# A two-block transformer layer on one core: output-stage tile order, routing's counts and slot table, and the first row gather

## The chip, the cores and the metric

The kernel runs as one program on one core of a Trainium2 chip. TensorE (PE) multiplies matrices, VectorE (DVE) and ScalarE (ACT) do elementwise work, GpSimd (POOL) here mostly starts indexed transfers, and SyncE (SP) starts the weight loads. The metric is the device time of one execution in microseconds (us). All data are fp32.

## The reference, cut to what matters

Two transformer blocks run one behind the other. The second works on 528 tokens: 16 meta tokens and the 512 of the input. The change touches its last part: the output projection of the mixer, and a mixture of experts.

```
h = h + z @ w_o                                   # 528 x 1024
u = rmsnorm(h, norm_ffn_g)
g_logits = u @ w_group + b_group                  # 4 groups
g_prob = softmax(g_logits);  p_grp, g_sel = top_1(g_prob)
e_logits = (u @ w_router + b_router)[group g_sel] # 8 experts of the group
p_exp, e_sel = top_2(softmax(e_logits))
gate = p_grp * p_exp / sum(p_exp)
expert = g_sel * 8 + e_sel                        # two per token, 32 experts
# the tokens of each expert are collected in blocks, each block runs
hid = silu(xe @ w1[e]) * (xe @ w3[e]);  yb = hid @ w2[e]
# and is added back to its tokens, times gate; then a last rmsnorm
```

## The kernel before

The program is a row of stages, each with code for each engine. `stage(eng, name)` ends one on an engine: it drains the engine, raises the semaphore `stage_done` and waits until POOL, PE, ACT and DVE have all raised it. SP only waits at places named in its code. Three stages matter.

**The output stage** (`out_pe`, `out_act`, `out_dve`). The 528 tokens are five tiles, `TOK_TILES`: four of 128 tokens and a last one of 16. `HN_JOBS` lists the jobs in token order: two halves of 512 columns for a large tile (`rows`), one job for the tile of 16 (`strips`, four strips of 256 columns beside one another on the array). PE multiplies by `WO` (L2458, L2470) and adds the residual by a product with the identity (L2463, L2473). ACT copies the result out of PSUM (L2520, L2523), squares and sums it (L2531) and forms the reciprocal root by Ln and Exp, with a table load for each (L2536, L2538). DVE multiplies by it and the gain (`UN`, L2560). PE turns `UN` (`turn`, L2483), DVE copies it (`turned`, L2554, `UT`), and PE multiplies by the router's weights (`logits`, L2491). `turn` and `logits` of a tile are queued behind products of later tiles. ACT stores `UN` in DRAM (`u_rows`, semaphore `u_stored`).

**Routing** (`route_dve`, `route_pe`, `route_act`), all of it behind the logits of the last tile. It is one chain of small DVE instructions; the helper `then` puts a drain behind an instruction, so that the next one starts when it has finished.

- DVE adds the bias (L2705), picks the group, and hands `GE` to ACT for an Exp (L2719 to L2722, the group's share of the gate).
- It picks two experts (L2725 to L2728 and the helper `first_best`, L2711 to L2715), and works out the gates `ga1` and `ga2` with a second Exp on ACT (L2731 to L2736). The gates are read first in the last stage.
- It forms the one-hot rows `ES` (L2738 to L2744). PE counts with 20 products of 32 columns how many rows of each expert come before each token (L2683, 15 products) and in all (L2686, 5).
- DVE works out, for each of the 1056 rows, a pair of experts and a slot in it: the rank, how often 64 rows are exceeded, a running sum over the experts in five steps (L2768, L2769), then the one-hot matrices `BH` and `AH` (L2787, L2788), multiplied by the token's number and by validity (L2793, L2794).
- PE multiplies them in 10 products (L2691), and DVE writes the table `BT` of token numbers (L2807). The lists for overflowing experts are formed while PE works (L2798 to L2805).

**The experts' stage** begins behind a barrier. 32 experts run in pairs, 64 rows each: 16 pairs, and more only where an expert overflows (none does here: the 1536 matmul records of L2872 are 16 times 96). POOL copies a column of `BT` (L2849) and gathers 128 rows (L2851); PE turns them (L2865) and multiplies by `w1`, `w3` and `w2` (L2872). There is one buffer for each of the three weights of each expert of the pair, 4 MB a pair. SP's loop (`pair`) loads the next `w1` when PE is through with this one (`h_one`, L2817), then `w3` (`h_done`, L2820) and `w2` (`y_done`, L2823). The first pair's weights are loaded earlier: `w1` in the output stage (L2826), `w3` and `w2` when the output stage is over and the rows are stored (L2830, L2832).

## Time and profile before

| | before |
|---|---|
| median of 3 runs | 2624.28 us (2615.44 to 2624.36) |
| the profiled execution | 2615.88 us, span 2614.0 us |
| PE busy | 2299.6 us (88%), 10135 matmul records |
| DVE busy | 963.9 us (37%) |
| ACT, POOL busy | 451.7 us (17%), 51.4 us (2%) |
| granted TensorE clock, mean | 0.94 |

The profiled execution lasted 1.88 us longer than its span. Shares are of the whole span, and say little of a stage of 80 us. Where the rows below name a time, it counts from the start of the span. In a row of the timeline, the square brackets give how long the engine was idle before it, and what released it.

### The profile page before, as it was taken

The page shows a single profiled execution, that of the slowest core. Times are in us where ns is not written, and L with a number is a line of the kernel's source. Part 1 is how long each engine was busy: PE and PEld are TensorE (multiplying, and loading weights), DVE is VectorE, ACT ScalarE, POOL GpSimd, SP SyncE. Part 2 cuts the span into 40 slices and gives each one's busy share as a digit, 9 for nine tenths or more (in the row PEclk, how much of TensorE's full clock was granted, in tenths as well). Part 3 has the DMA queues.
Part 4 walks back from the last instruction along what each step waited for, and adds up shares of the span by engine and source line. Part 5 has one row for each costly group of instructions (what it writes and reads, how often), then busy time and mean ns, then how long its engine had stood idle before and what let it go on. Part 6 is the DMA issues. An engine that isn't in the chain of part 4 may idle for free. (4 is left out here: it accounts for less than half of the span.)

```text
span 2614.0 us, 26286 instructions
## 1 busy us (share of the span) xinstructions
PE 2299.6 (88%) x10135; PEld 1567.2 (60%) x10135; DVE 963.9 (37%) x1964; ACT 451.7 (17%) x851; POOL 51.4 (2%) x76
## 2 busy tenths in 40 slices
PE   7999999989989999999989997788999487777783
PEld 5888887336644888887558774456875333232231
DVE  5455433133643555434310207867541400010003
ACT  2001001253451001001110014432113000000001
POOL 0000000000000000000000000000000000000001
PEclk9999999999999999999999987889999599899997
DMA  3233222111005323231132110000241399999996
GB/s 127 66 96 97 77 89 90 49 33 32 1 11 183 124 69 97 88 106 57 49 86 72 57 41 1 1 9 25 73 142 70 154 400 431 431 430 430 431 430 253
DMA packets 167750, 359.90 MB, mean 138 GB/s; under 512 B 15153, under 2 KB 143793, under 8 KB 155362
## 3 DMA queue, kind: packets, MB, share of 16 engines
q1 hardware_dynamic: 159136, 326.89, 33.6%
q0 software_dynamic: 5600, 21.10, 2.1%
q10 hardware_dynamic: 2914, 10.56, 1.0%
q8 instruction: 65, 1.06, 0.2%
q14 instruction: 35, 0.29, 0.0%
HBM read 337.49 MB, written 21.04 MB: 137 GB/s over the span
## 5 line engine op out<-in xcount | busy, mean ns | idle before, releaser
L575 PE MATMUL PS<-M 128*128 128x256 f32 x2464 | 542.2, 382 | 10.5 <-DVE M L324 7.3
L575 PEld LDWEIGHTS PS<-M 128*128 128x128 f32 x2464 | 469.4, 191 | 84.1 <-DMA M<-w_ffn_up 11.2
L2872 PE MATMUL PS<-M 128*64 128x512 f32 x1536 | 372.5, 641 | 100.2 <-DMA M<-w 76.7
L2872 PEld LDWEIGHTS PS<-M 128*64 128x64 f32 x1536 | 125.9, 147 | 335.4 <-issue 310.4
L606 PE MATMUL PS<-M 128*128 128x256 f32 x1232 | 268.7, 379 | 5.0 <-DVE M L690 2.5
L606 PEld LDWEIGHTS PS<-M 128*128 128x128 f32 x1232 | 233.4, 190 | 42.1 <-issue 10.7
L69 PE MATMUL PS<-M 128*128 128x264 f32 (+1 forms) x824 | 205.9, 412 | 22.1 <-ACT M L313 9.6
L69 PEld LDWEIGHTS PS<-M 128*128 128x128 f32 x824 | 158.9, 195 | 68.6 <-issue 21.4
L2938 DVE TENSOR_TENSOR M<-M,PS 128x512 f32<-128x512 f32 x16 | 11.0, 687 | 445.1 <-PE PS L2872 445.1
L693 DVE TENSOR_TENSOR M<-M,PS 128x256 f32<-128x256 f32 x220 | 92.6, 421 | 200.8 <-PE PS L575 196.7
L2289 PE MATMUL PS<-M 128*128 128x264 f32 x616 | 142.9, 394 | 8.0 <-DVE M L2388 5.1
L2289 PEld LDWEIGHTS PS<-M 128*128 128x128 f32 x616 | 118.5, 194 | 32.2 <-DVE M L2388 5.3
L349 PE MATMUL PS<-M 128*128 128x512 f32 x256 | 114.9, 612 | 9.6 <-POOLq L258 5.8
L349 PEld LDWEIGHTS PS<-M 128*128 128x128 f32 x256 | 50.2, 197 | 74.3 <-issue 72.8
L647 DVE TENSOR_TENSOR M<-M 128x512 f32<-128x512 f32 (+1 forms) x68 | 45.6, 671 | 126.1 <-DMA M<-w_ffn_down 110.4
L635 ACT ACTIVATE M<-M 128x256 f32<-128x256 f32 x66 | 27.5, 417 | 325.1 <-DVE M L693 325.1
L2924 ACT ACTIVATE M<-PS 128x1024 f32<-128x1024 f32 x16 | 16.4, 1023 | 356.9 <-PE PS L2872 356.9
L313 ACT ACTIVATE M<-M 128x512 f32<-128x512 f32 (+1 forms) x40 | 21.4, 618 | 226.1 <-DVEq L258 226.1
L2470 PE MATMUL PS<-M 128*128 128x512 f32 x128 | 56.5, 594 | 2.1 <-DVEq L258 2.1
L883 PE MATMUL PS<-M 128*128 128x512 f32 x128 | 56.4, 598 | 0.0
L1620 DVE TENSOR_TENSOR M<-PS,M 128x528 f32<-128x528 f32 x10 | 7.0, 705 | 126.6 <-PE PS L69 126.6
L650 DVE TENSOR_TENSOR M<-M 128x512 f32<-128x512 f32 (+1 forms) x68 | 46.0, 676 | 6.3
(362 smaller groups left out, 2273.9 us busy)
## 6 DMA issues: line engine op xcount, KB each, us to landing
M<-w SPq DMA_DIRECT2D x96, 2048.0 KB, 18.6
M<-w_ffn_gate SPq DMA_DIRECT2D x22, 1024.0 KB, 5.5
M<-w_ffn_up SPq DMA_DIRECT2D x22, 1024.0 KB, 5.3
M<-w_ffn_down SPq DMA_DIRECT2D x16, 1024.0 KB, 5.1
M<-w_in SPq DMA_DIRECT2D x13, 1024.0 KB, 5.3
M<-w_in SPq DMA_DIRECT2D x25, 512.0 KB, 3.9
expert_rows<-M POOLq DMA_DIRECT2D x2, 4096.0 KB, 24.3
expert_rows<-M ACTq DMA_DIRECT2D x16, 512.0 KB, 10.2
```

What stands on the lines that cost most here:

```text
L69: last = nc.tensor.matmul(PS[lo:lo + m, bank + c, 0:self.n], lhsT, rhs[:, c * self.n:(c + 1) * self.n], start=start, stop=stop)
L349: last = nc.tensor.matmul(PS[:, 4 + k, :], slot(s, 0, tiles, P)[:, a, :], rhs(a), start=a == 0, stop=a == tiles - 1)
L575: last = nc.tensor.matmul(PS[:, 3 * half + BANK[p], 0:HALF], lhs[:, a, :], rhs[:, a, :], start=p in FIRST and a == 0, stop=p in LAST and a ...
L606: last = nc.tensor.matmul(down_bank(name), lhs[:, c, :], rhs[lo + c], start=q == 0 and c == 0, stop=q == len(DOWN_PARTS) - 1 and c == n - 1)
L635: nc.scalar.activation(GQ[:, k, :], GQ[:, k, :], ACT.Silu).then_inc(activated, 1)
L647: nc.vector.tensor_tensor(wsum(m, "S1"), A(1, 0), A(1, 1), ALU.add).then_inc(weights_summed, 1)
L650: nc.vector.tensor_tensor(wsum(m, "S2"), wsum(m, "S1"), A(0, 0), ALU.subtract).then_inc(weights_summed, 1)
L693: nc.vector.tensor_tensor(dest, a, b, ALU.add).then_inc(block_taken, 1)
L883: last = nc.tensor.matmul(PS[:, bank, :], slot(s, k * KD * P, KD, P)[:, a, :], xnT[:, a, 0:S1], start=a == 0, stop=a == KD - 1)
L2289: last = nc.tensor.matmul(gbank(c, BANK[p]), lhs[:, a, :], rhs[:, a, :], start=p in ("P1", "P6", "P5") and a == 0, stop=p in ("P2", "P4", ...
L2470: nc.tensor.matmul(PS[:, n % 2, :], ZT[:, a, lo:lo + P], WO[:, a, 512 * half:512 * half + 512], start=a == 0, stop=False)
L2872: last = nc.tensor.matmul(PS[ROWS * k:ROWS * k + ROWS, bank, :], wide[:, a * P + ROWS * k:a * P + ROWS * k + ROWS], weights(k), start=star ...
```

## The change

It has four parts. (1) In the output stage the tile of 16 tokens goes first: the order is 4, 0, 1, 2, 3. (2) The counts come from six products over 192, 160, 128, 96, 64 and 32 columns in place of 20 over 32; DVE reads them in PSUM, and the running sum over the experts is replaced for this purpose by a comparison table `EARLIER`, formed while PE counts; the running sum itself and the overflow lists stand behind `BT`. (3) The gates' arithmetic, its two Exps too, stands behind the slot table. Only `AH` is multiplied, by one constant, and PE starts on the first choice's five products while DVE forms the second's. (4) POOL gathers the first rows when `BT` is written, ahead of the barrier.

```diff
-    c["c_tokid"] = (t.reshape(5, P).T - S2).astype(f).copy()
+    c["c_tokid"] = np.where(t < S2, t - S2, 0).reshape(5, P).T.astype(f).copy()
...
-        HN_JOBS = [(t, lo, w, half) for t, (lo, w) in enumerate(TOK_TILES) for half in range(2 if w == P else 1)]
+        ORDER = (4, 0, 1, 2, 3)
+        HN_JOBS = [(k, t, half) for k, t in enumerate(ORDER) for half in range(2 if TOK_TILES[t][1] == P else 1)]
...
-            for n, (t, lo, w, half) in enumerate(HN_JOBS):
+            for n, (k, t, half) in enumerate(HN_JOBS):
+                lo, w = TOK_TILES[t]
                 pe.wait_ge(hn_free, n + 1)
                 if w < P:
                     strips(n, lo, w)
                 else:
                     rows(n, lo, half)
-                if half == 0 and t >= 2:
-                    if t == 2:
+                if half == 0 and k >= 2:
+                    if k == 2:
                         pe.wait_ge(rw_in, 48)
-                    logits(t - 2)
-                if (half == 1 or w < P) and t >= 1:
-                    turn(t - 1)
+                    logits(k - 2)
+                if half == 1:
+                    turn(k - 1)
...
+            def store(k):
+                lo, w = TOK_TILES[ORDER[k]]
+                act.wait_ge(un_ready, k + 1)
+                act.dma_start(u_dram[lo:lo + w, :], UN[0:w, ORDER[k], :]).then_inc(u_stored, 16)
...
+                last.then_inc(hn_free, 1)
+                if w == P and half == 0:
+                    store(k - 1)
+                    continue
...
+            for k, t in enumerate(ORDER):
+                w = TOK_TILES[t][1]
+                if k == 4:
+                    turned(3)
+                dve.wait_ge(rs5, k + 1)
                 nc.vector.scalar_tensor_tensor(UN[0:w, t, :], HN[0:w, t, :], C5["rs"][0:w, t:t + 1], GROW[0:w],
                                                ALU.mult, ALU.mult).then_inc(un_ready, 1)
-                if t > 0:
-                    turned(t - 1)
+                if 0 < k < 4:
+                    turned(k - 1)
...
-            for t in range(5):
-                for b in range(t + 1):
-                    nc.tensor.matmul(PS[:, 0, 32 * t:32 * t + 32], C["before"] if b == t else ones, ES[:, b, :],
-                                     start=b == 0, stop=b == t)
-            for t in range(5):
-                last = nc.tensor.matmul(PS[:, 1, 0:32], ones, ES[:, t, :], start=t == 0, stop=t == 4)
+            columns = ES.rearrange("p t e -> p (t e)")
+            nc.tensor.matmul(PS[:, 0, 0:192], C["before"], columns, start=True, stop=False)
+            for k in range(1, 6):
+                last = nc.tensor.matmul(PS[:, 0, 32 * k:192], ones, columns[:, 0:192 - 32 * k], start=False, stop=k == 5)
             last.then_inc(e_counted, 1)
-            pe.wait_ge(slots_ready, 1)
-            for n in range(10):
-                j, t = n % 2, n // 2
-                last = nc.tensor.matmul(PS[:, 2, 0:PAIRS], BH[:, j, t * P:(t + 1) * P],
-                                        AH[:, j, t * PAIRS:(t + 1) * PAIRS],
-                                        start=n == 0, stop=n == 9)
+            for j in range(2):
+                pe.wait_ge(slots_ready, j + 1)
+                for t in range(5):
+                    last = nc.tensor.matmul(PS[:, 2, 0:PAIRS], BH[:, j, t * P:(t + 1) * P],
+                                            AH[:, j, t * PAIRS:(t + 1) * PAIRS],
+                                            start=j == t == 0, stop=j == 1 and t == 4)
             last.then_inc(buf_ready, 1)
...
-            tt(GE, G, bc(C5["gmax"], 4), ALU.subtract).then_inc(ge_in, 1)
-            dve.wait_ge(ge_out, 1)
-            then(nc.vector.reduce_sum(C5["gsum"], GE, axis=AX))
-            then(nc.vector.reciprocal(C5["gsum"], C5["gsum"]))
...
-            tt(C5["ex"], C5["m2"], C5["m1"], ALU.subtract).then_inc(ex_in, 1)
-            dve.wait_ge(ex_out, 1)
-            then(ts_(C5["den"], C5["ex"], 1.0, None, ALU.add))
-            then(nc.vector.reciprocal(C5["den"], C5["den"]))
-            then(tt(C5["ga1"], C5["gsum"], C5["den"], ALU.mult))
-            then(tt(C5["ga2"], C5["ga1"], C5["ex"], ALU.mult))
...
-            per_expert("pair", C["pair0"])
-            per_expert("half", C["half0"])
-            dve.wait_ge(e_counted, 1)
-            nc.vector.tensor_copy(PRE, PS[:, 0, 0:160].rearrange("p (t e) -> p t e", t=5))
-            then(nc.vector.tensor_copy(CNT, PS[:, 1, 0:32]))
-            per_expert("rank", PRE)
...
+            then(per_expert("pair", C["pair0"]))
+            then(per_expert("half", C["half0"]))
+            ts_(C10["step"], C10["pair"], -1.0, float(BASE - 1), ALU.mult, ALU.add)
+            then(stt(C10["eid"], C10["half"], float(BASE) / ROWS, C10["pair"], ALU.mult, ALU.add))
+            tt(EARLIER, over(C["iota"][:, 0:32], 10), bc(C10["eid"], 32), ALU.is_lt)
+
             q80 = CMP[:, 0:80].rearrange("p (a m) -> p a m", m=8)
             n256 = CMP[:, 128:384].rearrange("p (a m) -> p a m", m=8)
             dve.wait_ge(u_stored, 96)
+            dve.wait_ge(e_counted, 1)
+            tt(T96, E12, PS[:, 0, 0:160].rearrange("p (t e) -> p t e", t=5).unsqueeze(1).to_broadcast([P, 2, 5, 32]),
+               ALU.mult)
+            then(tt(n256, bc(PS[:, 0, 160:192], 8), over(STEP64, 32), ALU.is_gt))
+            nc.vector.reduce_sum(by_choice(C10["rank"]), T96, axis=AX)
+            then(nc.vector.reduce_sum(NOV, n256, axis=AX))
             tt(q80, bc(C10["rank"], 8), over(STEP64, 10), ALU.is_ge)
-            then(tt(n256, bc(CNT, 8), over(STEP64, 32), ALU.is_gt))
+            then(tt(flat96, EARLIER, over(NOV, 10), ALU.mult))
             nc.vector.reduce_sum(C10["q"], q80, axis=AX)
-            then(nc.vector.reduce_sum(NOV, n256, axis=AX))
+            then(nc.vector.reduce_sum(by_choice(C10["ob"]), T96, axis=AX))
+            stt(C10["in"], C10["q"], -float(ROWS), C10["rank"], ALU.mult, ALU.add)
+            stt(C10["half"], C10["q"], 0.0, C10["half"], ALU.is_equal, ALU.mult)
+            tt(C10["step"], C10["step"], C10["q"], ALU.add)
+            dve.drain()
+            then(tt(C10["ob"], C10["ob"], C10["step"], ALU.add))
+            tt(C10["in"], C10["in"], C10["half"], ALU.add)
+            then(stt(C10["ob"], C10["q"], 0.0, C10["ob"], ALU.is_gt, ALU.mult))
+            then(tt(C10["pair"], C10["pair"], C10["ob"], ALU.add))
+            for j in range(2):
+                B = BH[:, j, :].rearrange("p (t s) -> p t s", t=5)
+                A = AH[:, j, :].rearrange("p (t b) -> p t b", t=5)
+                tt(A, over(C["iota"][:, 0:PAIRS], 5), bc(C10["pair"][:, 5 * j:5 * j + 5], PAIRS), ALU.is_equal)
+                then(tt(B, over(C["iota"], 5), bc(C10["in"][:, 5 * j:5 * j + 5], P), ALU.is_equal))
+                tt(A, A, bc(C["tokid"], PAIRS), ALU.mult).then_inc(slots_ready, 1)
+
+            tt(GE, G, bc(C5["gmax"], 4), ALU.subtract).then_inc(ge_in, 1)
+            tt(C5["ex"], C5["m2"], C5["m1"], ALU.subtract).then_inc(ex_in, 1)
+            stt(DI, C10["pair"], float(P), C10["in"], ALU.mult, ALU.add)
+            dve.wait_ge(ge_out, 1)
+            then(nc.vector.reduce_sum(C5["gsum"], GE, axis=AX))
+            nc.vector.reciprocal(C5["gsum"], C5["gsum"])
+            dve.wait_ge(ex_out, 1)
+            then(ts_(C5["den"], C5["ex"], 1.0, None, ALU.add))
+            dve.wait_ge(buf_ready, 1)
+            ts_(BT, PS[:, 2, 0:PAIRS], float(S2), None, ALU.add).then_inc(rows_named, 1)
+
+            then(nc.vector.reciprocal(C5["den"], C5["den"]))
+            then(tt(C5["ga1"], C5["gsum"], C5["den"], ALU.mult))
+            tt(C5["ga2"], C5["ga1"], C5["ex"], ALU.mult)
             then(nc.vector.tensor_copy(BE[0], NOV))
...
-            then(tt(OB, ends, NOV, ALU.subtract))
-            per_expert("ob", OB)
-            then(stt(C10["ob"], C10["ob"], float(BASE - 1), C10["q"], ALU.add, ALU.add))
...
-            stt(DI, C10["pair"], float(P), C10["in"], ALU.mult, ALU.add)
-            for j in range(2):
-                B = BH[:, j, :].rearrange("p (t s) -> p t s", t=5)
-                A = AH[:, j, :].rearrange("p (t b) -> p t b", t=5)
-                tt(B, over(C["iota"], 5), bc(C10["in"][:, 5 * j:5 * j + 5], P), ALU.is_equal)
-                tt(A, over(C["iota"][:, 0:PAIRS], 5), bc(C10["pair"][:, 5 * j:5 * j + 5], PAIRS), ALU.is_equal)
-            dve.drain()
-            for j in range(2):
-                B = BH[:, j, :].rearrange("p (t s) -> p t s", t=5)
-                A = AH[:, j, :].rearrange("p (t b) -> p t b", t=5)
-                tt(B, B, bc(C["tokid"], P), ALU.mult)
-                tt(A, A, bc(C["valid"], PAIRS), ALU.mult)
-            dve.drain().then_inc(slots_ready, 1)
...
+        def gather_rows(pool, b):
+            nc.gpsimd.tensor_copy(IDX, BT[:, b:b + 1] if isinstance(b, int) else BT[:, ds(b, 1)])
+            pool.drain()
+            nc.gpsimd.indirect_dma_start(
+                out=XG, out_offset=None, in_=u_dram,
+                in_offset=bass.IndirectOffsetOnAxis(ap=IDX.bitcast(U32), axis=0)).then_inc(g_in, 16)
+        def first_rows_pool(pool):
+            pool.wait_ge(u_stored, 96)
+            pool.wait_ge(rows_named, 1)
+            gather_rows(pool, 0)
...
-            stage(pool, "pool")
+            first_rows_pool(pool); stage(pool, "pool")
```

PE at the end of the output stage (L2458 and L2463 are the tile of 16, L2483 a turn, L2491 logits). Before:

```order
L2458 MATMUL PS<-M 16x256 [waits hn_free]
L2458 MATMUL PS<-M 16x256 x31
L2463 MATMUL PS<-M 16x128 x8
L2491 MATMUL PS<-M 128x36 [waits ut_out]
L2491 MATMUL PS<-M 128x36 x7
L2483 MATMUL PS<-M 128x128 [waits ut_out,un_ready]
L2483 MATMUL PS<-M 128x128 x7
L2491 MATMUL PS<-M 128x36 [waits ut_out]
L2491 MATMUL PS<-M 128x36 x7
L2483 MATMUL PS<-M 128x16 [waits ut_out,un_ready]
```

The same place in the changed kernel, where L2471 and L2474 are the products of a large tile, L2485 a turn and L2494 logits:

```order
L2471 MATMUL PS<-M 128x512 [waits hn_free]
L2471 MATMUL PS<-M 128x512 x7
L2474 MATMUL PS<-M 128x128 x4
L2485 MATMUL PS<-M 128x128 [waits ut_out,un_ready]
L2485 MATMUL PS<-M 128x128 x7
L2494 MATMUL PS<-M 128x36 [waits ut_out]
L2494 MATMUL PS<-M 128x36 x7
L2485 MATMUL PS<-M 128x128 [waits ut_out,un_ready]
L2485 MATMUL PS<-M 128x128 x7
L2494 MATMUL PS<-M 128x36 [waits ut_out]
```

The small tile's products have left the end; its turn and logits too, and the last turn and the last logits are now those of a tile of 128.

PE in routing, before (L2683 and L2686 count, L2691 forms the table, L2865 turns the first gathered rows):

```order
L2683 MATMUL PS<-M 128x32 [waits e_onehot,stage_done]
L2683 MATMUL PS<-M 128x32 x14
L2686 MATMUL PS<-M 128x32 x5
L2691 MATMUL PS<-M 128x32 [waits slots_ready]
L2691 MATMUL PS<-M 128x32 x9
L2865 MATMUL PS<-M 128x128 [waits g_in,stage_done]
```

And in the changed kernel:

```order
L2691 MATMUL PS<-M 128x192 [waits e_onehot,stage_done]
L2693 MATMUL PS<-M 128x160
L2693 MATMUL PS<-M 128x128
L2693 MATMUL PS<-M 128x96
L2693 MATMUL PS<-M 128x64
L2693 MATMUL PS<-M 128x32
L2698 MATMUL PS<-M 128x32 [waits slots_ready]
L2698 MATMUL PS<-M 128x32 x4
L2698 MATMUL PS<-M 128x32 [waits slots_ready]
L2698 MATMUL PS<-M 128x32 x4
L2878 MATMUL PS<-M 128x128 [waits g_in,stage_done]
```

Twenty counting products have become six, and the ten of the table have a wait in their middle. On DVE, the changed kernel's first rows behind the table (L2796 writes `BT`, L2798 to L2800 end the gates, L2801 begins the running sum):

```order
L2791 TENSOR_REDUCE M<-M 128x5 [waits ge_out]
L2792 RECIPROCAL M<-M 128x5
L2794 TENSOR_SCALAR M<-M 128x5 [waits ex_out]
L2796 TENSOR_SCALAR M<-PS 128x32 [waits buf_ready]
L2798 RECIPROCAL M<-M 128x5
L2799 TENSOR_TENSOR M<-M 128x5
L2800 TENSOR_TENSOR M<-M 128x5
L2801 COPY M<-M 128x32
```

Before, `BT` (L2807) was the last instruction of the stage; now 23 instructions of DVE stand between it and the barrier.

## Rows read from the trace of the kernel before

**Rows 1.** Chain that ended last, experts' stage: start, us, what.

```profile
2075.73 4.45 DMA M<-u_rows,M
...
2083.83 16.36 PE PS L2872 x64
...
2119.42 8.77 PE PS L2872 x32
...
2562.38 8.80 PE PS L2872 x32
```

**Rows 2.** Timeline of SP's queue: start, us, queue, line, transfer.

```profile
2039.16 0.80 SPq L2830 DMA_DIRECT2D M<-w  x2
...
2093.49 0.88 SPq L2817 DMA_DIRECT2D M<-w  x2
```

**Rows 3.** Windows: us, busy of PE, PEld, DVE, ACT, POOL, PEclk, DMA share, GB/s.

```profile
2043.00:2058.00 15.00, 8.71 (x40) 8.61 (x40) 6.36 (x27) 0.21 (x1) 0.00 (x0) 0.50 1.01 428
...
2093.00:2562.00 469.00, 371.50 (x1622) 139.51 (x1618) 37.64 (x45) 24.90 (x31) 16.09 (x28) 0.93 1.01 428
```

**Rows 4.** Timeline, end of the output stage: start us, us, engine, line, operation.

```profile
2020.57 0.60 ACT L2523 ACTIVATE M<-PS 128x512 f32<-128x512 f32 x1 [8.95 <-PE PS L2473]
...
2021.34 3.65 PE L2458 MATMUL PS<-M 128*16 128x256 f32 x64
...
2024.35 1.28 DVE L2560 SCALAR_TENSOR_TENSOR M<-M 128x1024 f32<-128x1024 f32 x1 [15.70 <-ACT M L2536]
...
2025.55 1.28 DVE L2554 COPY M<-PS 128x512 f32<-128x512 f32 x2
...
2026.92 1.98 PE L2491 MATMUL PS<-M 128*128 128x36 f32 x16 [1.49 <-DVEq L2556]
...
2028.72 1.07 PE L2483 MATMUL PS<-M 128*128 128x128 f32 x8
...
2032.88 3.63 PE L2491 MATMUL PS<-M 128*128 128x36 f32 x16 [3.08 <-DVEq L2556]
...
2037.95 1.14 PE L2491 MATMUL PS<-M 128*16 128x36 f32 x16 [0.48 <-DVEq L2556]
```

**Rows 5.** Timeline, routing up to the counts.

```profile
2039.20 0.68 DVE L2705 TENSOR_TENSOR M<-PS,M 128x36 f32<-128x36 f32 x5 [1.33 <-POOLq L258]
...
2041.23 0.18 DVE L2719 TENSOR_TENSOR M<-M 128x20 f32<-128x20 f32 x1
...
2042.27 0.33 DVE L2725 TENSOR_TENSOR M<-M 128x160 f32<-128x160 f32 x1
...
2046.18 0.17 DVE L2731 TENSOR_TENSOR M<-M 128x5 f32<-128x5 f32 x1
...
2047.60 0.18 DVE L2738 TENSOR_TENSOR M<-M 128x20 f32<-128x20 f32 x1
2047.86 0.56 DVE L2740 TENSOR_TENSOR M<-M 128x160 f32<-128x160 f32 x2
...
2049.05 6.58 PE L2683 MATMUL PS<-M 128*128 128x32 f32 x30 [9.96 <-DVE M L2744]
...
2057.79 0.33 DVE L2755 COPY M<-PS 128x160 f32<-128x160 f32 x1 [6.80 <-PE PS L2686]
```

**Rows 6.** Page, costliest groups: busy us, mean ns, idle before.

```profile
L575 PE MATMUL PS<-M 128*128 128x256 f32 x2464 | 542.2, 382 | 10.5 <-DVE M L324 7.3
```

**Rows 7.** Timeline, slot table and the start of the first gather.

```profile
2069.84 4.47 PE L2691 MATMUL PS<-M 128*128 128x32 f32 x20 [12.09 <-DVEq L2795]
...
2074.35 0.19 DVE L2807 TENSOR_SCALAR M<-PS 128x32 int32<-128x32 f32 x1 [1.60 <-PE PS L2691]
...
2074.69 0.19 POOL L2849 COPY M<-M 128x1 int32<-128x1 int32 x1 [285.78 <-DVEq L258]
```

**Rows 8.** DVE groups by line, 2000 to 2150: busy us, mean ns, idle.

```profile
L2748 DVE TENSOR_TENSOR M<-M 128x320 f32<-128x320 f32 x4 | 2.0, 491 | 0.2
...
L2787 DVE TENSOR_TENSOR M<-M 128x640 f32<-128x640 f32 x2 | 1.6, 820 | 0.0
```

More of the change, by code:

```diff
@@ L2536, in out_act @@
                 nc.scalar.activation(C5["rs"][0:w, t:t + 1], C5["rs"][0:w, t:t + 1], ACT.Exp, scale=-0.5).then_inc(rs5, 1)
-                if t < 4:
+                if k < 4:
                     nc.scalar.preload_act_table_set(LN)
-            for t in (3, 4):
-                lo, w = TOK_TILES[t]
-                act.wait_ge(un_ready, t + 1)
-                act.dma_start(u_dram[lo:lo + w, :], UN[0:w, t, :]).then_inc(u_stored, 16)
+            store(4)
         def out_dve(dve):
@@ L2630, in program @@
         T96, E12 = at(RG0 + 4096, 2, 5, 32), at(RG0 + 4416, 2, 5, 32)
-        T48, ES, PRE = T96[:, 0], at(RG0 + 4736, 5, 32), at(RG0 + 4896, 5, 32)
-        CNT, NOV, OB = small(32), small(32), small(32)
+        T48, ES, EARLIER = T96[:, 0], at(RG0 + 4736, 6, 32), at(RG0 + 5120, 10, 32)
+        NOV = small(32)
         BE = [small(32), small(32)]
         C5 = {n: small(5) for n in ("gmax", "gsum", "mx", "m1", "m2", "ex", "den", "ga1", "ga2", "ss", "rs")}
-        C10 = {n: small(10) for n in ("rank", "pair", "half", "ob", "q", "in", "out")}
+        C10 = {n: small(10) for n in ("rank", "pair", "half", "ob", "q", "in", "eid", "step")}
         STEP64 = small(8)
@@ L2705, in route_dve @@
                 tt(LG[0:w, t, :], PS[0:w, 6, 36 * t:36 * t + 36], g["router_bias"][0:w], ALU.add)
+            nc.vector.memset(ES[:, 5, :], 0.0)
             dve.drain()
@@ L2743, in route_dve @@
             dve.drain()
-            tt(ES, E12[:, 0], E12[:, 1], ALU.add).then_inc(e_onehot, 1)
+            tt(ES[:, 0:5, :], E12[:, 0], E12[:, 1], ALU.add).then_inc(e_onehot, 1)
             def per_expert(name, values):
```

86 lines of the change are left out of this document (34 added, 52 removed).

## The prediction, made before the changed kernel was run

> **What bounds the kernel now.** I read the chain that ended last first, from its end backwards, since it says which stages have a price. From the first pair to the last it goes through weight transfers and TensorE in turn: the `w3` products of the first pair run in a piece that begins at 2083.83, those of the second pair begin at 2119.42 and the last pair's at 2562.38 [rows 1], which is 14 periods of 31.64 us. The windows show why: from 2093 to 2562 the DMA share is 1.01 at 428 GB/s [rows 3]. The loop is bound by the transfer of 12.6 MB of weights a pair, and it starts when SP's first looped load is issued, at 2093.49 [rows 2], which the first pair's `w1` products release. No later piece of the chain is tied to a fixed time. So what is taken off ahead of 2093.49 comes off the end, us for us, as long as nothing else takes its place.
>
> Ahead of it the chain runs back over the first gather (2075.73, 4.45 us to landing [rows 1]) to the barrier and the chain of DVE and TensorE in routing. From DVE's first instruction (2039.20 [rows 5]) to the gather's issue it is 36.5 us, in which TensorE has its low level (granted clock 0.50, 1.2 GHz [rows 3]). The second thing that runs there is the load of `w3` and `w2` of the first pair, issued at 2039.16 [rows 2]: 8.4 MB at the 428 GB/s of the window are 19.6 us, so they end near 2060, 15 us before the gather is issued. That is the cover, and the change eats nearly all of it.
>
> **Part 1, the tile order.** The last large product ended at 2020.57, where ACT copies it; DVE has its reciprocal root at 2024.35, 3.78 us later [rows 4]. In the changed kernel the same product comes later by the small tile's products (3.65 us for the strips [rows 4], about 0.45 for the identity's 16 records at the same rate), its turn (at most the 1.07 of a full one) and its logits (1.14 at the low clock [rows 4]; I take 0.7 at the high one): 5.8 us in all, so 2026.4. Then 3.78 to the root (2030.1), `UN` 1.28, turn 1.07, DVE's copies 1.28, logits 1.98 [rows 4], and 0.2 for the steps between: the last logits end at 2035.9. Before, they ended at 2037.95 + 1.14 = 2039.09 [rows 4]. **Gain 3.2.** The doubt is the clock. The same 16 logits records took 1.98 behind a pause of 1.49, and 3.63 behind one of 3.08 [rows 4]. In the new order the pauses near the end are 1.3, 0.7 and 1.3, each with work between, so I take 1.98; with 3.63 the gain is 1.5. The added release of `hn_free` costs nothing: two jobs may run ahead of it. Of the stores, the last is now 512 KB, issued at about 2031.5; POOL, SP and DVE wait for it, all of them later than 2036.
>
> **Part 2a, the gates behind the table.** From L2719 to L2725 it is 1.04 us, from L2731 to L2738 1.42 us [rows 5], and both leave the chain. A memset adds 0.06. **Gain 2.4.** They return behind the second choice's matrices, while TensorE multiplies for 3 us, and behind `BT`.
>
> **Part 2b, the counts.** Before, 40 records take from 2049.05 to 2057.79, 0.219 each [rows 5]: they are set by something other than their 32 columns. Twelve records at that price would be 2.6 us. A record of 256 columns took 542.2 / 2464 = 0.220 us at nearly the full clock [rows 6], 0.86 ns a column and 1.72 at half of it, so 192 and 160 columns cost 0.33 and 0.275, and the sum is 2 x (0.33 + 0.275) + 8 x 0.22 = 2.97 us. I take that. Meanwhile DVE has four instructions of 320 columns and three new ones (`step`, `eid`, `EARLIER`) to do, which end 2.9 us after the counts begin; the two finish together. **Gain 8.74 - 2.97 = 5.8**, less 0.1 for that race: 5.7.
>
> **Part 2c, from counts to table.** Prices: 0.17 for 5 to 20 columns, 0.33 for 160 [rows 5], 0.49 for 320, 0.82 for 640 [rows 8], and by the same line 0.24 for 80 and 0.43 for 256. Behind a drain the next begins 0.08 after the end (2047.60 + 0.18 to 2047.86), without one 0.08 before it (two of 0.32 in 0.56 [rows 5]). Operands in PSUM cost nothing more: 160 columns took 0.33 from there [rows 5].
> - Eight instructions up to `q` and `ob`: 4 x 0.49 + 2 x 0.43 + 2 x 0.24 = 3.3, the steps cancel.
> - Seven of 10 columns: 1.25.
> - First choice: 0.32 + 0.82 + 0.32, 1.45. So `slots_ready` rises 6.0 us behind the counts, and the second time 1.4 later.
> - Ten products of two records: 4.47 us [rows 7]. The second five are queued behind the first five and their data are there, so TensorE ends at 10.5.
>
> Before, it is 2074.35 - 2057.79 = 16.56 [rows 5, 7]. **Gain 6.1**: 4.7 from DVE's chain, 12.05 before (2057.79 to 2069.84), since the running sum and two multiplications of 640 columns are gone from it, and 1.4 from TensorE's start on the first choice.
>
> **Part 3, the gather ahead of the barrier.** POOL waits for `rows_named` in place of the barrier. Before, `BT` ended at 2074.54 and POOL's copy began at 2074.69 [rows 7]: **gain 0.05 to 0.1**. What this part really does is to hide what now stands behind `BT`. DVE's tail: the gates' three small ones (0.6), the copy and five steps of the running sum (0.25 + 5 x 0.33, two overlapped small ones and a drain each), two comparisons (0.15), one of 512 columns (0.77), a reduction of 512 (0.77), four small ones (0.7): 4.9 us behind `BT`'s start. The barrier opens at 5.0. The gathered rows came 2080.18 - 2074.35 = 5.8 behind `BT`'s start [rows 1, 7]. So the tail is covered, with 0.8 us to spare; without the part it would cost all of its 4.9. Late next is the gather itself, as before, and everything after it is as before, with a first pair that begins at the low clock (2083.83, 16.36 us [rows 1]).
>
> **The sum**: 3.2 + 2.4 + 5.7 + 6.1 + 0.1 = 17.5 us. Against the profiled execution's own 2615.88 that is 2598.4. The three timed runs lie at 2615.44, 2624.36 and 2624.28: the profiled one is like the first, and 8.4 under the median. Against the median the sum gives 2606.8. Nothing in one trace says which of these the changed kernel's median will be like, so I name the middle, **2603**, and keep both for the range.
>
> **Rivals.**
> - *GpSimd is held up by DVE.* Before, POOL copied and issued with DVE idle; now DVE's tail runs beside it. What it could cost is bounded: nothing, or that the copy and the issue wait for the whole tail, so that the gather's 4.45 us begin at about 6.4 (5.0 and the 1.4 from copy to issue) in place of 1.4, and land 5.0 us later: 12.5 saved, 2603.4 by its own time. The gathers inside the loop run beside single DVE instructions and speak for little. [...] Since no instruction of the tail is longer than 0.69 and there are drains between them, I take part of it as possible, 1 to 5 us. Chance 0.17.
> - *The weights' loads become the bound of the gather.* They start 3.2 us earlier and the gather 17.5 earlier, so the distance shrinks from 15 us to about 1.2 (it is what parts 2 and 3 save, 14.3, that counts). If routing saves over 1.2 us more than I say, or the loads are issued late, the gather moves beside the end of `w2`. It decides for at most 1 to 2 us: saved 16, 2600. Chance 0.08.
> - *TensorE falls to the low clock in the output tail*, or DVE's steps cost more than priced: 14 to 16 saved, 2601. Chance 0.1.
> - *Slower: the loop's period grows.* The loop starts at another moment, and it is 15 periods long. A period of 31.64 us [rows 1] longer by 1.17 us, 3.7%, takes back all 17.5; the DMA rings are full, and the rate of 428 GB/s [rows 3] would have to fall to 413. The 8.9 us between the runs of before, if they lie in the loop, are 0.6 us a period, half of that. At twice the spread and a little, 1.25 us a period, the time is 2598.4 + 18.8 = 2617.2, slower than before's own 2615.9. Against it: the order and size of what is moved in the loop do not change. Chance 0.03.
> - *It does not shorten the chain*, because a transfer or a store released the experts' stage. The trace excludes that: the barrier's last arrival was DVE, and the loads were over 14 us before.
>
> **How the numbers follow.** My forecast (16.5 to 18.5 saved) has 0.62. Measurement tells about 0.5% from no change, 13.1 us. The forecast is beyond it, by 4 us; if before and after are drawn from opposite ends of the spread of 8.9 it is not, or it is nearly twice as much. Before's median is already the high end, which leaves mostly the good side. Of the first rival half stays beyond 13.1, of the second and third nearly all by the sum, less one part in ten for the spread. Faster 0.77, same 0.20, slower 0.03. Range: the low end is 2615.44 less 20 (the sum with the counts at 2.6 us and DVE's steps 2 us below my prices), 2595, and the high end is 2624.36 less the 12.5 of the first rival at its full price, 2612; three runs show a spread only from inside, so I add 3 on both sides: 2592 to 2615.
>
> **What the profile will show.** L2471's last product and L2712 (DVE's first in routing) 3 us earlier than L2705 was; L2691 and L2693 as 12 records in 3.0 us; DVE's L2763 right at their end; L2698 in two groups, with no gap between them; `BT` (L2796) about 21 us behind L2712, where it was 35.2 behind L2705; POOL's copy within 0.1 of it; the rows landed 0.5 to 1 us behind the barrier; periods of 31.6. I would be wrong if POOL's issue stretches beside DVE's tail, if the barrier comes after the rows, if 3.63 us stand for the last logits, or if the periods change.

## The result

| | before | changed |
|---|---|---|
| median, first comparison | 2623.68 us (2615.44 to 2629.89, 9 runs) | 2607.2 us (2603.49 to 2616.51, 9 runs) |
| ratio, first comparison | | 0.9947, interval 0.9935 to 0.996 |
| median, second comparison | 2619.79 us (2611.66 to 2627.22, 15 runs) | 2608.43 us (2605.11 to 2612.61, 10 runs) |
| ratio, second comparison | | 0.9961, interval 0.9946 to 0.9977 |
| the profiled execution | 2615.88 us, span 2614.0 | 2608.14 us, span 2606.3 |

The changed kernel is faster, by 10 to 14 us of 2620 as the two ratios have it, and so right at the bound of 0.5% that I had named.

**The profile after.** The page's first lines, the spans being 7.7 us apart:

```profile
span 2606.3 us, 26222 instructions
PE 2296.7 (88%) x10107; PEld 1562.3 (60%) x10107; DVE 961.7 (37%) x1961; ACT 451.5 (17%) x851; POOL 51.0 (2%) x76
```

7.7 us is not the gain. The output stage began later in this execution than in the one of before, ahead of any instruction that was changed. The first product of that stage in the timeline of before (start, us, engine, line):

```profile
1952.87 1.55 PE L2470 MATMUL PS<-M 128*128 128x512 f32 x3 [2.13 <-DVEq L258]
```

and in the chain of the changed kernel (start, us, what), with the last large product, ACT's and DVE's steps behind it, the last turn and the last logits:

```profile
1957.99 3.65 PE PS L2459 x64
...
2030.38 0.90 PE PS L2474 x8
2031.31 0.60 ACT M L2533
...
2035.08 1.29 DVE M L2568
2036.42 1.98 PE PS L2485 x8
2038.42 0.69 DVE M L2559
...
2039.80 3.64 PE PS L2494 x16
2043.54 0.67 DVE M L2712 x5
```

So I measure from that first product to the issue of the first looped weight load, a stretch that holds all that was changed: 2093.49 - 1952.87 = 140.62 us before [rows 2], and 2084.41 - 1957.99 = 126.42 after. The rest of routing in the timeline of the changed kernel:

```profile
2050.96 0.98 PE L2691 MATMUL PS<-M 128*128 128x192 f32 x2 [7.53 <-DVE M L2741]
...
2051.73 2.29 PE L2693 MATMUL PS<-M 128*128 128x160 f32 x10
...
2054.13 0.49 DVE L2763 TENSOR_TENSOR M<-M,PS 128x320 f32<-128x320 f32 x1 [0.34 <-PE PS L2693]
...
2060.06 4.48 PE L2698 MATMUL PS<-M 128*128 128x32 f32 x20 [6.04 <-DVE M L2785]
...
2064.57 0.19 DVE L2796 TENSOR_SCALAR M<-PS 128x32 int32<-128x32 f32 x1 [2.28 <-PE PS L2698]
...
2064.92 0.19 POOL L2858 COPY M<-M 128x1 int32<-128x1 int32 x1 [270.90 <-DVE M L2796]
...
2065.96 1.06 POOL L2860 DMA_INDIRECT M<-u_rows,M  x1 [0.85 <-issue]
...
2069.52 0.18 DVE L2817 TENSOR_SCALAR M<-M 128x34 int32<-128x34 f32 x1
2070.77 1.28 ACT L2930 ACT_TABLE_LOAD   x1 [8.90 <-POOLq L258]
...
2070.81 1.97 PE L2878 MATMUL PS<-M 128*128 128x128 f32 x8 [6.27 <-POOLq L258]
...
2084.41 0.88 SPq L2827 DMA_DIRECT2D M<-w  x2
```

Read with rows 4, 5 and 7 this gives the gain piece by piece, each a difference of two starts:

| piece | before | changed | gain | predicted |
|---|---|---|---|---|
| first product of the output stage to DVE's first in routing | 86.33 | 85.55 | 0.8 | 3.2 |
| from there to the first count | 9.85 | 7.42 | 2.4 | 2.4 |
| first count to the table's instruction | 25.30 | 13.61 | 11.7 | 11.8 |
| table to the turn of the first rows | 5.96 | 6.24 | -0.3 | 0.1 |
| turn to the first looped load | 13.18 | 13.60 | -0.4 | 0 |
| sum | 140.62 | 126.42 | 14.2 | 17.5 |

The second and third lines came as worked out. The last two are 0.4 us short each: the rows were turned 4.85 us behind the gather's issue and not 4.58, and turn to load is taken up under e2. The first line lacks most, 2.4 us, and the chain shows what took it: the last turn took 1.98 and not 1.07, and the last logits 3.64 and not 1.98. The windows of the changed kernel (us, busy of the engines, granted clock, DMA share, GB/s) show why:

```profile
2031.00:2034.00 3.00, 1.59 (x15) 1.35 (x14) 1.29 (x2) 2.49 (x5) 0.00 (x0) 1.00 0.00 0
2034.00:2036.00 2.00, 1.53 (x14) 1.42 (x13) 0.92 (x1) 1.04 (x2) 0.00 (x0) 0.91 0.00 0
2036.00:2038.00 2.00, 1.58 (x8) 1.57 (x8) 0.37 (x1) 0.00 (x0) 0.00 (x0) 0.50 0.39 162
```

The mean of 0.91 over the two us from 2034 puts the fall to the low level, 1.2 GHz, at about 2035.6. TensorE had then had a pause of 1.41 us, 1.98 us of logits (2033.56 to 2035.54), and the first 0.1 us of a pause of 0.89. No pause was as long as the 3.08 us of before. And that pause, from 2029.79 to 2032.88, was longer than the fall needed. The window of before there:

```profile
2030.00:2031.00 1.00, 0.00 (x0) 0.00 (x0) 0.68 (x1) 0.28 (x2) 0.00 (x0) 0.83 0.96 393
```

A mean of 0.83 puts the fall at 2030.7, 0.9 us into the pause.

### The profile page after: what moved, and what is told of

It reads as the page before. It is cut to its first block, busy times and chain, and to the rows that moved or that the text cites. A ratio compares the mean times of both kernels' runs of the same rounds, so it can differ in the third digit from the quotient of the medians.

```text
span 2606.3 us, 26222 instructions
## 1 busy us (share of the span) xinstructions
PE 2296.7 (88%) x10107; PEld 1562.3 (60%) x10107; DVE 961.7 (37%) x1961; ACT 451.5 (17%) x851; POOL 51.0 (2%) x76
## 4 chain that ended last, share of the span: by engine, by line
PE 45%; DMA 15%; DVE 5%; DVEq 2%; ACT 1%; issue 1%; SPq 0%; POOLq 0%; ACTq 0%; POOL 0%
DMA M<-w 13%; PE PS L575 9%; PE PS L69 7%; PE PS L2885 6%; PE PS L2289 5%; PE PS L349 4%; PE PS L606 4%; PE PS L2471 2%; DMA M<-w_ffn_up 2%; PE PS L1563 1%; DVE M L1880 1%; DVEq L1884 1%; PE PS L2044 1%; PE PS L1800 1%; PE PS L460 1%
## 5 line engine op out<-in xcount | busy, mean ns | idle before, releaser
L2471 PE MATMUL PS<-M 128*128 128x512 f32 x128 | 56.7, 596 | 0.0
```

The lines of the kernel that those rows point to most:

```text
L2471: nc.tensor.matmul(PS[:, n % 2, :], ZT[:, a, lo:lo + P], WO[:, a, 512 * half:512 * half + 512], start=a == 0, stop=False)
```

## The experiments

All kernels are the changed one with an edit. The stretch is that of above; `start` is the first product of the output stage. I read nothing from times of whole executions where there is only one, for a reason that the table shows: the starts differ by 12 us in code that is the same in all of them. For completeness, the single times were 2607.70 (e1), 2611.58 (e2), 2606.43 (e3) and 2605.77 us (e4) beside 2627.76 for the kernel before, 2607.95 (e5), 2611.86 (e6) and 2608.52 (e7) beside 2622.05, and 2609.63 (e9) and 2621.05 (b9).

| kernel | start | output stage | to count | count to table | table to turn | turn to load | stretch | load to end |
|---|---|---|---|---|---|---|---|---|
| before | 1952.87 | 86.33 | 9.85 | 25.30 | 5.96 | 13.18 | 140.62 | 520.5 |
| before, again (b9) | 1958.20 | 86.32 | 9.86 | 25.30 | 5.84 | 13.26 | 140.58 | 520.4 |
| changed | 1957.99 | 85.55 | 7.42 | 13.61 | 6.24 | 13.60 | 126.42 | 521.9 |
| changed, again (a9) | 1957.99 | 85.55 | 7.43 | 13.62 | 6.02 | 13.78 | 126.40 | 520.9 |
| e1, order of before | 1957.16 | 86.32 | 7.43 | 13.61 | 6.21 | 13.34 | 126.91 | 521.8 |
| e2, twenty counts | 1958.08 | 85.55 | 7.43 | 19.26 | 6.33 | 12.52 | 131.09 | 520.5 |
| e3, gates ahead | 1956.53 | 85.55 | 9.89 | 13.62 | 6.22 | 12.53 | 127.81 | 520.3 |
| e4, gather behind | 1953.04 | 85.56 | 7.44 | 13.61 | 11.19 | 12.95 | 130.75 | 520.1 |
| e5, POOL arrives first | 1957.37 | 85.54 | 7.43 | 13.61 | 6.22 | 13.66 | 126.46 | 522.3 |
| e6, spares in the output tail | 1964.57 | 83.02 | 7.43 | 13.62 | 6.25 | 13.26 | 123.58 | 521.9 |
| e7, spares everywhere | 1965.13 | 83.02 | 7.34 | 11.47 | 7.49 | 9.96 | 119.28 | 522.3 |
| e8, spares, fewer at the end | 1960.45 | 83.03 | 7.34 | 11.49 | 6.67 | 10.00 | 118.53 | 519.1 |
| e9, order of before, spares | 1963.37 | 83.85 | 7.44 | 13.62 | 6.23 | 12.79 | 123.93 | 520.5 |

**e1: the tile order of before.** The edit puts `HN_JOBS`, `out_pe`, `out_act` and `out_dve` of before in place of the new ones.

```diff
-        ORDER = (4, 0, 1, 2, 3)
+        HN_JOBS = [(t, lo, w, half) for t, (lo, w) in enumerate(TOK_TILES) for half in range(2 if w == P else 1)]
...
```

> Measure for all these runs: the stretch from TensorE's first product of the output stage to the issue of the first looped weight load. It is 140.6 us in the kernel before and 126.4 in the changed one. Theory: the new tile order is worth 0.8 us and not 3.2, because its last turn and last logits run at the low clock; with the order of before the output stage (first product to DVE's first instruction of routing) takes 86.3 us in place of 85.6, and the stretch is 127.2. Rival, my prediction's term: the stretch is 129.6.

The output stage took 86.32 us, 0.77 more than in the changed kernel. The order is worth 0.8 us. The stretch is 126.91; the steps behind the output stage ran 0.3 us shorter here, nearly all of it between the turn and the load.

**e2: twenty counting products.**

```diff
-            nc.tensor.matmul(PS[:, 0, 0:192], C["before"], columns, start=True, stop=False)
-            for k in range(1, 6):
-                last = nc.tensor.matmul(PS[:, 0, 32 * k:192], ones, columns[:, 0:192 - 32 * k], start=False, stop=k == 5)
+            for t in range(5):
+                for b in range(t + 1):
+                    nc.tensor.matmul(PS[:, 0, 32 * t:32 * t + 32], C["before"] if b == t else ones, ES[:, b, :],
+                                     start=b == 0, stop=b == t)
+            for t in range(5):
+                last = nc.tensor.matmul(PS[:, 0, 160:192], ones, ES[:, t, :], start=t == 0, stop=t == 4)
```

> The changed kernel with twenty counting products of 32 columns. Theory: the six products are worth 8.74 - 2.97, less 0.1: DVE's wait for the counts ends 5.7 us later, the stretch is 132.1. Rival: what was gained behind the counts came from DVE's new instructions alone and half of the 5.7 is hidden by them; the stretch is 129.

From the first count to the table it is 19.26 in place of 13.61: the six products are worth 5.65 us, as the theory has it (its 5.7), and not half. The timeline shows the same 30 and 10 records as before:

```profile
2051.06 6.58 PE L2693 MATMUL PS<-M 128*128 128x32 f32 x30 [7.54 <-DVE M L2744]
2057.45 2.32 PE L2696 MATMUL PS<-M 128*128 128x32 f32 x10
```

The stretch is 131.09 and not 132.1, since turn to load was 12.52 in this execution. That piece is 12.5 to 13.8 in kernels that do the same there. It holds the moment at which the clock rises inside the first pair's `w1` products. By the windows it rose 7.0 us behind the turn's start in e2, 9.2 and 9.6 in the two executions of the changed kernel (13.60 and 13.78), and 8.4 in before (13.18); over the eleven executions without spare products there, the order of these moments is the order of the pieces. What sets the moment was not tried.

**e3: the gates ahead.** The block from `tt(GE, ...)` to `den`, and the three instructions behind `BT`, stand where they stood before.

```diff
             first_best(G, C5["gmax"], C["g4"], 4, OHG)
+            tt(GE, G, bc(C5["gmax"], 4), ALU.subtract).then_inc(ge_in, 1)
+            dve.wait_ge(ge_out, 1)
+            then(nc.vector.reduce_sum(C5["gsum"], GE, axis=AX))
+            then(nc.vector.reciprocal(C5["gsum"], C5["gsum"]))
...
```

> The changed kernel with the gates' arithmetic and both Exps back in their old places. Theory: 2.4 us more ahead of the counts, and nothing comes back behind the table, where DVE waits for TensorE anyway: the stretch is 128.8. Rival: the shorter tail behind the table opens the barrier 0.6 us earlier and the first products with it; 128.2.

To the first count it is 9.89 in place of 7.42: 2.5 us. Nothing changed behind the table (13.62, 6.22), so the shorter tail gave nothing back: the rival falls. The stretch is 127.81 and not 128.8, since turn to load is 12.53 here, as in e2.

**e4: the first gather behind the barrier.**

```diff
-            first_rows_pool(pool); stage(pool, "pool")
+            stage(pool, "pool"); first_rows_pool(pool)
```

> The changed kernel with the first gather behind the barrier. Theory: the gather is issued 5.1 to 5.2 us later, behind DVE's tail, and everything after it shifts: the stretch is 131.5. Rival: the gather beside DVE's tail is slowed (its rows took 4.7 us to land, 4.45 in the kernel before), so alone it lands 0.25 faster and the shift is 4.9: 131.3. A third, that the barrier waits for GpSimd's drain until the rows are there, says that here the barrier opens 5.2 us behind the table in place of 6.2.

```profile
2059.65 0.19 DVE L2796 TENSOR_SCALAR M<-PS 128x32 int32<-128x32 f32 x1 [2.28 <-PE PS L2698]
2064.58 0.18 DVE L2817 TENSOR_SCALAR M<-M 128x34 int32<-128x34 f32 x1
2064.86 1.28 ACT L2930 ACT_TABLE_LOAD   x1 [7.91 <-DVEq L258]
2064.90 0.19 POOL L2858 COPY M<-M 128x1 int32<-128x1 int32 x1 [275.92 <-DVEq L258]
2065.94 1.04 POOL L2860 DMA_INDIRECT M<-u_rows,M  x1 [0.85 <-issue]
2070.84 1.52 PE L2878 MATMUL PS<-M 128*128 128x128 f32 x6 [11.22 <-DMA M<-u_rows,M]
```

The turn comes 11.19 us behind the table in place of 6.24. The early gather is worth 4.95 us, next to nothing against before (0.1 predicted) but all of DVE's tail that was put there. The rows were turned 4.90 us behind the gather's issue here, with DVE idle, against 4.85 with DVE's tail beside it. So the tail did not slow the gather. And the barrier opened 5.21 us behind the table, where the changed kernel's opened at 6.20 and named POOL's queue as what released it. That led to the next.

Of e1 to e4 this kernel had the shortest time (2605.77, against 2607.7, 2611.58 and 2606.43), with a stretch 4.3 us longer than the changed kernel's: its output stage began at 1953.04, 3.5 us and more ahead of the others'.

**e5: POOL arrives at the barrier ahead of its gather.**

```diff
+            if isinstance(b, int):
+                pool.drain().then_inc(stage_done, 1)
+            else:
+                pool.drain()
...
-            first_rows_pool(pool); stage(pool, "pool")
+            first_rows_pool(pool)
+            n = stage_no["pool"] = stage_no["pool"] + 1
+            pool.wait_ge(stage_done, WORKERS * n)
```

> GpSimd raises the barrier's semaphore between its copy and its gather, in place of behind the gather. In the changed kernel the barrier opened 6.20 us behind the start of the table's instruction, 1.1 behind DVE's last. Theory: GpSimd's drain waited for the rows, so the barrier now opens at 5.2 to 5.3; TensorE then starts when the rows land (4.45 to 4.7 behind the issue, 5.85 to 6.1 behind the table) and gains 0.1 to 0.3 us. Rival: the barrier opens as late as before, since it was something else; no gain.

```profile
2063.95 0.19 DVE L2796 TENSOR_SCALAR M<-PS 128x32 int32<-128x32 f32 x1 [2.28 <-PE PS L2698]
...
2069.18 1.28 ACT L2933 ACT_TABLE_LOAD   x1 [7.92 <-DVEq L258]
2070.17 1.95 PE L2881 MATMUL PS<-M 128*128 128x128 f32 x8 [6.26 <-DMA M<-u_rows,M]
```

The barrier opened at 5.23 us, released by DVE: half of the theory holds. POOL's drain does wait until the rows are there, or close to it. In eight executions with the drain behind the gather (all of the changed kernel's and its variants' but e4, e5 and e7) the barrier opened at 5.99 to 6.64, always 0.03 or 0.04 us ahead of the turn. The gain did not come (6.22 against 6.24), because the rows themselves are not there sooner. The name of the releaser changed, and the time did not.

**e6: spare products in the output tail.** They multiply two constants into the eighth PSUM bank and are read by nobody.

```diff
+        def spare(n):
+            for _ in range(n):
+                nc.tensor.matmul(PS[:, 7, 0:P], ident, C["before"], start=True, stop=True)
...
+            spare(5)
             logits(3)
+            spare(3)
             turn(4)
+            spare(5)
             logits(4)
```

> 13 products whose result nobody reads (128 columns, 0.22 us each at the high clock, into a bank that nothing uses) fill TensorE's last three pauses in the output stage. Theory: the clock stays high, the last turn takes 1.05 in place of 1.97 and the last logits 1.98 in place of 3.63, the output stage takes 83.0 us in place of 85.6, the stretch is 123.9. Rival: the clock falls for another reason than the pauses (small products count as little activity); the turn and logits stay as slow and the stretch is 126.4 to 127.

```profile
2041.95 0.91 PE L2457 MATMUL PS<-M 128*128 128x128 f32 x6
2043.01 1.09 PE L2489 MATMUL PS<-M 128*128 128x128 f32 x8
2043.94 1.28 PE L2457 MATMUL PS<-M 128*128 128x128 f32 x10
2045.51 1.98 PE L2498 MATMUL PS<-M 128*128 128x36 f32 x16 [0.29 <-DVEq L2568]
```

The turn took 1.09 and the logits 1.98, and the output stage 83.02 us, 2.5 less. That is the whole of what the prediction missed in part 1. The cause is the clock, which stayed at 1.00 in every window from 2040 to 2048, and filling the pauses was enough to hold it here. All three were filled at once, so which of them mattered is not shown.

**e7: spare products everywhere.** As e6, and 30 ahead of the counts, 25 between counts and table, 25 behind the table's products.

```diff
+            spare(30)
             pe.wait_ge(e_onehot, 1)
...
+            spare(25)
             for j in range(2):
                 pe.wait_ge(slots_ready, j + 1)
...
             last.then_inc(buf_ready, 1)
+            spare(25)
```

> As e6_spare_out, and 30, 25 and 25 more such products ahead of the counts, between counts and table, and between table and the first rows. Theory: at the high clock the counts take 1.5 us (3.0 before, but DVE's own work ends at 2.9, so 0.1 is gained), the table's products end 2.0 us earlier, the first pair's products take 13.6 in place of 16.75, of which w1's half starts the loop 2.5 to 3 us earlier: the stretch is 119. Rival: the clock falls all the same, the spare products take twice as long, 13 us ahead of the counts, and delay them by 5 us or more: the stretch is 130 or more.

The stretch is 119.28, near the theory's 119, by two misses that cancel. Count to table fell from 13.61 to 11.47, turn to load from 13.60 to 9.96, more than the 2.5 to 3 expected. But table to turn rose from 6.24 to 7.49, and the timeline says that TensorE was the last at the barrier:

```profile
2066.76 7.46 PE L2457 MATMUL PS<-M 128*128 128x128 f32 x50
...
2074.26 1.28 ACT L2940 ACT_TABLE_LOAD   x1 [8.19 <-PEq L258]
2074.45 1.13 PE L2888 MATMUL PS<-M 128*128 128x128 f32 x8 [0.23 <-PEq L258]
```

Its 25 spare products took 7.46 us, 0.30 each, where the 25 ahead of the table took 5.83, 0.23 each: by the windows the clock fell just behind their start, at 2066.8, and was low until 2070.2.

**e8: fewer at the end.** `spare(30)`, `spare(31)`, `spare(18)`.

> As e7_spare_all with 30, 31 and 18 spare products in place of 30, 25 and 25. In e7 TensorE itself came to the barrier 7.3 us behind the table, since its last 25 spare products took 7.46 us. Theory: 18 are over before the rows land, TensorE turns them 6.25 us behind the table in place of 7.49, the clock stays high through the table's products, and the stretch is 118.0, 8.4 less than in the changed kernel; the time is 8 us below it, 0.9915 to 0.993 of the kernel before. Rival: the first pair's last load, which starts 2.5 us earlier while the gather starts 4.3 us earlier, now overlaps the gather, whose rows land 1 to 2 us later: the stretch is 119 to 120, and the ratio 0.993 to 0.995.

The turn comes at 6.67, and the stretch is 118.53, between the two expectations. The rival accounts for 0.4 us of it: the windows of e8 show the last load of `w2` still running when the gather was issued at 2063.70, and the turn came 5.28 behind that issue, in place of 4.85. No run has the overlap alone, so that it is the cause is argued, not shown.

```profile
2056.00:2062.00 6.00, 5.85 (x52) 5.55 (x50) 4.96 (x22) 0.32 (x2) 0.00 (x0) 1.00 1.01 429
2062.00:2064.00 2.00, 2.00 (x12) 2.00 (x12) 1.32 (x10) 0.00 (x0) 0.49 (x2) 0.52 1.01 434
2064.00:2066.00 2.00, 2.00 (x13) 2.00 (x13) 1.68 (x12) 0.00 (x0) 0.77 (x1) 0.62 0.56 164
```

The same windows show what I had not expected: the clock fell at 2062.1, with every pause filled. The timeline of TensorE there:

```profile
2052.33 7.17 PE L2457 MATMUL PS<-M 128*128 128x128 f32 x62
...
2059.59 2.69 PE L2707 MATMUL PS<-M 128*128 128x32 f32 x20
...
2062.09 5.89 PE L2457 MATMUL PS<-M 128*128 128x128 f32 x36
```

The longest pause in the 18 us ahead of the fall was 0.39 (at 2050.8), and the last thing done was the table's 2.69 us of products of 32 columns. The clock was low until 2065.5, in the spare products, where it delayed nothing: they were over 1.0 us before the turn. So spare products held the clock in the output tail (e6), up to the counts and up to the table, but filled pauses are not enough everywhere. Why it fell here stays open.

Its median is 2597.1 us (2595.39 to 2600.43, 6 runs), 0.9916 of the kernel before, interval 0.9897 to 0.9935. That is 22.0 us of 2620, and the stretch is 22.1 shorter. It beats both kernels; the changed one, run beside it on the same chip, had 0.9961. Between those two the medians differ by 11.3 us and the stretches by 7.9, so some of that difference lies outside the stretch: load to end, for one, was 1.8 us shorter in e8's trace than in a9's.

**a9: the changed kernel once more.**

> The changed kernel once more, on the same chip as e8_spare_tuned. Theory: the stretch is 126 to 127 again and the ratio to the kernel before 0.994 to 0.996, since the stretch is 14 us shorter and nothing else is changed. Rival: the 16.5 us between the medians is the gain, and some of it lies outside the stretch; the ratio is 0.9935 or less.

The stretch is 126.40, the ratio 0.9961, a hair above the theory's 0.994 to 0.996, with an interval of 0.9946 to 0.9977 that leaves the rival's 0.9935 out. The medians are 11.4 us apart here and were 16.5 the first time, with a stretch 14.2 us shorter both times. So about 5 us of such a difference are the spread of whole executions; that the starts make it up is likely, since they differ by 12 us, but not shown.

**e9: order of before, with spares.** 5 of them behind the products of the small tile, 12 ahead of the logits of the last large one.

```diff
+                if w < P:
+                    spare(5)
...
+            spare(12)
             logits(3)
             turn(4)
             logits(4)
```

> The changed kernel with the tile order of before and 5 and 12 spare products in the two long pauses of that order's tail. Theory: with the clock held the logits of the last large tile take 1.98 in place of 3.63, the output stage takes 84.6 us in place of 86.3, so the new order is worth 1.6 us at the held clock (83.0 in e6_spare_out) and 0.8 where the clock falls. Rival: spare products delay the tail's own; 86 or more.

The output stage took 83.85 us, less than I expected, since the small tile's turn and logits are faster too at the high clock. Against 83.02 with the new order, the order is worth 0.8 us whether the clock is held or not; the 1.6 of the expectation is wrong.

**b9: the kernel before once more.**

> The kernel before once more, for its trace. In its first trace the gathered rows were turned 4.58 us behind the gather's issue, in the changed kernel and its variants 4.8 to 4.9, with and without DVE beside it. Theory: that is the spread of executions, and here it is anywhere from 4.5 to 4.9; the stretch is 140 to 141.5. Rival: it is a property of the changed kernels, and here it is 4.6 again. Ahead of the output stage the executions differ by up to 12 us (first product at 1953 to 1965 us), which this one should fall into as well.

The stretch is 140.58. The rows were turned 4.47 us behind the issue (4.58 the first time), in the nine changed kernels without spare products ahead of the turn it was 4.64 to 4.94, and in e8 5.28. So a part of it, 0.2 to 0.3 us, seems to belong to the changed kernels, though a9's 4.64 is nearly before's. It is neither DVE's tail (e4) nor the drain of POOL (e5). What it is stays open.

## Why the prediction was right, and where it was off

**Where the chain is, and that it shifts us for us: right.** From the first looped load to the end it was 520.4 and 520.5 us in the two traces of before and 520.1 to 522.3 in ten of the changed kernels (e8: 519.1). So the loop gave back 0 to 2 us. What decides this is not shown. In the first pair of traces it was 1.4, and the last pair's `w2` products alone make 1.7: they took 8.81 us and not 7.11. The windows of the changed kernel and of before have the clock of that piece:

```profile
2562.00:2574.00 12.00, 9.53 (x36) 3.17 (x36) 1.38 (x2) 0.76 (x1) 0.00 (x0) 0.86 0.00 0
```

```profile
2571.00:2581.00 10.00, 8.00 (x38) 2.77 (x36) 1.38 (x2) 0.23 (x1) 0.00 (x0) 1.00 0.01 2
```

**Part 1: the size was wrong.** The step that failed is the clock in the output tail, "so I take 1.98; with 3.63 the gain is 1.5": I had 3.2 us, and it was 0.8. I had placed the last large product 73.5 us behind the stage's start, and it ended at 73.3; the root came 3.77 behind that. But the clock was low from the last turn on, which I had priced for the logits alone, and the gain was 0.8 (e1), not 1.5. I read the clock's fall from the one pause of 3.08 us, and took a row of short pauses with work between for safe. The window of before could have warned me: the clock fell 0.9 us into that pause. e6 shows that filling the three pauses of 1.4, 0.9 and 1.4 us held it, and gave 2.5 us. My 3.2 had compared the new order at the high clock with the old one at the low. The order alone is worth 0.8 at either (e1, e9); the rest was a clock that it did not hold.

**Parts 2a, 2b and 2c: right,** 2.4 (e3: 2.5), 5.7 (e2: 5.65), and 11.7 for the two pieces of counts and table together against 11.8. A DVE chain of small instructions can be priced from their durations and two gaps: from the counts' arrival (2054.13) to the table's first product (2060.06) it was 5.93 us, and I had 6.0. The six products took 3.17 against 2.97, DVE waited 0.34 for them.

**Part 3: right in what it hides** (e4: 4.95, for a tail that I had at 4.9), and wrong in what opens the barrier. I had not seen that POOL's drain in front of the barrier lasts until the gather is nearly done. It cost nothing (e5).

**The first rival fell.** The gather's issue took 1.06 us beside DVE's instructions and 1.04 with DVE idle (before and e4), and its rows were turned 4.85 us behind the issue in the changed kernel and 4.90 in e4. The Trainium skill ("SBUF — State Buffer", Who interferes with whom) has a DVE instruction in a two-port mode, such as a copy can enter, block GpSimd while it runs. It adds that a DVE copy was seen to stall such a transfer and a two-input `tensor_tensor` was not. That agrees with these runs as far as they go: the tail's copies are short, 0.15 to 0.18 us, and its 23 instructions of at most 0.69 us behind the table cost the gather nothing that can be seen. A long copy beside a gather was not tried.

**The second rival** decided nothing in the changed kernel. Its margin was misreckoned: 15 less 14.3 is 0.7 and not 1.2, and with the 19.6 us counted from the loads' issue [rows 2] it would have been 2.7. The loads were over before the gather was issued: behind 2064 only 0.29 MB were left of them, and the gather came at 2065.96. In e8, where the margin was used up, the rows came 0.4 us later.

**The third rival, to which I had given 0.1, is what happened:** TensorE fell to the low clock in the output tail, 3.63 us stood for the last logits, which I had named as a sign of being wrong, and 14.2 us were saved, within its 14 to 16 and not within the 16.5 to 18.5 of my forecast.

**The slower rival** did not occur: from the second pair's piece in the chain to the last pair's it is 443.03 us (2110.13 to 2553.16), where before it was 442.96 [rows 1].

**The numbers.** The sum was 17.5, the trace has 14.2. Of the 3.3 us between them 2.4 are part 1's, 0.4 the gathered rows', 0.4 the later rise of the clock behind the turn, and 0.1 the counts'. The ratios of 0.9947 and 0.9961 are 13.9 and 10.2 us of 2620. Luck has a share in how near the first time came. That the first two medians lie 16.5 us apart, close to the sum, is the spread of executions; the second two lie 11.4 apart. My 2603 was the middle of 2598.4 and 2606.8, and the 2607.2 lies at the second of these although 3.3 us of the sum were missing. I had given 0.77 to a change beyond 0.5%; both intervals, 0.9935 to 0.996 and 0.9946 to 0.9977, have 0.995 in them, so that is not settled.

## What to carry to other kernels

Sum instructions as here, but ask for each TensorE piece in a sparse stretch what it costs at either clock level, and take the low one unless a trace shows that pattern of pauses at the high one. Where TensorE waits in a chain of small steps, products that nobody reads are a cheap way to hold the clock, though not a sure one (e8 lost it for 3.4 us), and here were worth 8 us, over half as much as the whole change; their number must be bounded by the pause, since what overhangs delays the next real one. And when a gain is 0.5% of a long kernel, measure a stretch of the trace between two fixed instructions around the edit, which repeated to 0.04 us here in both kernels that were traced twice, while the start of that stretch moved by 12. Read it piece by piece all the same: turn to load differed by 1.3 us between kernels that are alike there.

## What the runs showed of the hardware

- The clock fell after a stretch in which no pause was over 1.41 us: a pause of 1.41, 1.98 us of logits, and 0.1 us of the next pause. In the kernel before it fell 0.9 us into a pause. With the pauses of the tail filled to 0.29 or less it stayed at 1.00 through the whole tail (e6).
- In e8 it fell with no pause over 0.39 us in the 18 us before, behind 2.69 us of products of 32 columns, and rose again 3.4 us later under products of 128 columns. Why is open.
- GpSimd's drain behind an indexed transfer lasted until about when the rows landed: the barrier opened 6.20 us behind the table with it, and 5.23 without.
- Code that is the same in 13 traces reached the output stage between 1952.87 and 1965.13 us. The two kernels that were latest, e6 and e7, ran on one chip together with e5, which had 1957.37; whether the chip, the moment or the code decides was not tried.
